# Attention heads of a two-layer diffusion block: projection blocks one step later, maxima first, other banks, early output projection

## The chip, the cores and the metric

One Trainium2 chip, one core of it. The metric is the time of one execution on the device in microseconds (us), median of several runs. All arithmetic is float32; a product of weights is made from three passes (see below). Engines: PE multiplies matrices (a weight load, PEld, goes with each product), DVE and ACT work on vectors, POOL is a third vector engine, SP only issues the transfers of weights (DMAs). Each has its own queue and runs it in order; they wait for each other by semaphores. Products land in eight banks (bank 0 to 7) of 128 x 512 numbers.

## The reference

Two layers over 256 context and 256 latent tokens of width 1024. Layer 0 is attention with compressed queries and keys/values, layer 1 a chunked state-space scan; a gated FFN follows each. The change lies in layer 0's attention alone:

```
proj = h @ w_in;  cq, ckv, kr = split(proj, [512, 768])
q  = rms_norm(cq)  @ w_uq      # 16 heads x (64 plain + 32 rotary)
kv = rms_norm(ckv) @ w_ukv     # 16 heads x (64 keys + 64 values)
q_rope, kr: rotated by position, latent tokens only
per head: s = (q k^T) / sqrt(96);  p = softmax(s);  o = p @ v
   latent queries see all 512 tokens, context queries the 256 of the context
out = concat(o) @ w_o          # 1024 x 1024
x = x + gate * out             # then norm and FFN
```

## The kernel before

Activations lie transposed (channels on partitions, tokens along the row). A weight block of 128 x 1024 (or 512) numbers comes by DMA into one of four `raw` buffers; ACT copies its high part into `w_hi` (`hi`, L574), DVE subtracts for `w_lo` (`lo`, L993), and PE makes three products for each of them (`three`, L1551 to L1553: low x high, high x high, high x low). The ring has four slots: a block's `hi` waits until the block four before is used (`w_used`), SP's load until its `w_lo` is written. Results of each sub-layer are split into high and low in the same way.

Layer 0's attention runs head by head. The queries and keys of four heads come from four projection blocks: K (keys of four heads, two halves of six products), C (rotary part of four queries, 12 products), A and B (plain part of two heads each, 12 products). `HEAD_BLOCKS` gives their order, K C A B for heads 0 to 3 and then A B C K for each group. Blocks 0 to 4 are done ahead of the loop, block i+5 in step i.

Step i of the loop (`head(i)`, written out for each engine in its own function) holds:

- PE: scores of head i+1 in three products (`scores`, L1737 and L1741; banks 0, 1, 4), transposes of head i's probabilities in three parts (`transpose_probs`, L1752 and L1756; banks 5, 6, 2), the swap of rotary halves in steps 2, 6, 10 (`swap`, L1723; bank 7), a projection block (bank 7; a K block in banks 5 and 6, whose halves first wait for the copies of the transposes there, `pt_out`), and the values of head i (`values`, L1768 and L1771; bank 3, after `pt_out` of the third part and after the low halves of head i-1, `o_lo`).
- ACT: exponentials of head i+1 (`exps`, L782 and L787) and copies of the transposed probabilities (`pt_split`, L799) by turns, copies of the projection block out of its bank (`project_out`: keys L751, rotary L756 and L761, plain L768), the next `hi`, the high halves of head i's output (L814).
- DVE: maxima of head i+1 (`maxes`, L1164 to L1170), inverses of the sums (`inverse`, L1178), the rotation in steps 2, 6, 10 (`rotate`, L1149 to L1157, reads bank 7), else a pair of matrix-vector operations for the modulation (`matvec`, L1070), the low halves of head i's output (L1195, reads bank 3), the next `lo`.
- POOL: three multiplies of the probabilities by the inverses (`scale_probs`, L460 to L464).
- SP: the load of the next head block or of an output projection block, and one vector-weight load.

After step 15 PE waits for the last low halves and makes the output projection: eight tiles of 128 channels, 24 products each; five over all tokens (banks 0 and 1 by turns), three in two halves. DVE adds each to the residual (L1222).

```
def head(i):                          # PE, before
    scores(i + 1, 0..2)
    transpose_probs(i, 0..2)          # for p < 2 of the step after a K block: wait k_out
    if i in ROPE_STEPS: swap(i + 4, bank[7])
    K: wait pt_out 3i+1; k_tile(b, 0, bank[5]); wait pt_out 3i+2; k_tile(b, 1, bank[6])
    else: q_tile(b, bank[7])          # b = i + 5
    values(i)
```

Of the kernel before, what the change touches and what calls it, by code (L numbers as in the profile page):

```python
# [27 lines left out]
CTX = 256  # L28
LAT = 256
# [73 lines left out]
HEAD_BLOCKS = [("K", 0), ("C", 0), ("A", 0), ("B", 0)] + [(kind, g) for g in range(1, 4) for kind in "ABCK"]  # L103
ROPE_STEPS = [b - 4 for b, (kind, g) in enumerate(HEAD_BLOCKS) if kind == "C" and g]
# [40 lines left out]
def program(nc, a, out):  # L145
# [9 lines left out]
    with ExitStack() as fixed:  # L155
# [407 lines left out]
        def _(act):  # L563
# [173 lines left out]

            def project_out(b, banks):
# [3 lines left out]
                if kind == "K":  # L742
                    for half in range(2):
                        if half:
                            act.wait_ge(w_used, HP + b + 1)
                        else:
                            act.wait_ge(k_mm, g + 1)
                        if g:
                            act.wait_ge(s_mm, 3 * h)
                        for u in range(2):  # L750
                            A(kf[0:64, 2 * half + u, :], banks[half][64 * u:64 * u + 64, :], ACT.Copy).then_inc(k_out, 1)  # L751
# [49 lines left out]
            def head(i):  # L801

                for p in (0, 1):
                    if i < 15:
                        exps(i + 1, p)
                    pt_split(i, p)
                pt_split(i, 2)
                if i < 15:
                    exps(i + 1, 2)
                if i + 5 < 16:  # L810
                    project_out(i + 5, (bank[5], bank[6]) if HEAD_BLOCKS[i + 5][0] == "K" else (bank[7],))
# [7 lines left out]
            project_out(3, (bank[2],))  # L819
            for p in range(3):  # L820
                exps(0, p)
            project_out(4, (bank[7],))
# [161 lines left out]
        def _(dve):  # L984
# [158 lines left out]
            def rotate(g, b):  # L1143
# [7 lines left out]
                V.tensor_tensor(rope_s[:, :], b[:, 0:LAT], tabv("sin", LAT), MUL).then_inc(rope_part, 1)  # L1151
# [27 lines left out]

            def head(i, v):  # L1180
                if i < 15:
                    maxes(i + 1, 0)
                    maxes(i + 1, 1)
                    inverse(i + 1, 0)
                    maxes(i + 1, 2)
                    inverse(i + 1, 1)
                if i in ROPE_STEPS:
                    rotate(HEAD_BLOCKS[i + 4][1], bank[7])
# [4 lines left out]
                for r in range(2):  # L1193
                    dve.wait_ge(o_hi, 2 * i + r + 1)
                    V.tensor_tensor(halves(Ol, i // 2, i % 2, r), bank[3][64 * r:64 * r + 64, 0:256].rearrange("p (s t) -> p s t", s=2),  # L1195
                                    halves(Oh, i // 2, i % 2, r).bitcast(f32), SUB).then_inc(o_lo, 1)
                if i + 5 < 16:
# [960 lines left out]
```

## Time and profile before

| | us |
|---|---|
| median of 3 runs | 1287.66 (1285.13 to 1290.57) |
| the profiled execution | 1290.45 |
| its span, first to last instruction | 1288.7 |
| busy PE / DVE / ACT / POOL | 1181.0 / 862.5 / 588.1 / 220.6 |
| mean granted TensorE clock | 0.963 |

The span is one profiled execution; sums made from its rows stand against 1290.45. Busy times say how full an engine is, not which wait decides; for that there is the chain of waits and, for one stretch, the timeline of each engine. A timeline row has the start, the duration, the engine and line, the operation and its shapes, how many were merged, and in brackets how long the engine was idle before it and who ended that. The granted clock is 1.00 at 2.4 GHz and 0.50 at 1.2 GHz.

### The profile page before, as it was taken

How to read it: one execution, taken by the hardware profiler on the slowest of the kernel's cores; microseconds unless marked ns; L12 is line 12 of the kernel's file. 1: busy time of each engine (PE TensorE's matmuls, PEld its weight loads, DVE VectorE, ACT ScalarE, POOL GpSimd, SP SyncE). 2: the span in 40 equal slices, each digit the busy share in tenths (PEclk: the TensorE clock that was granted, in tenths of full speed). 3: DMA queues.
4: the chain of work that ended last, by engine and by line, in shares of the span. 5: the costliest groups of instructions: out<-in, count | busy, mean ns of one | idle time of the engine just before them, and what ended most of it. 6: DMA issues, size and time to landing. Idle time of an engine off the chain costs nothing.

```text
span 1288.7 us, 19417 instructions
## 1 busy us (share of the span) xinstructions
PE 1181.0 (92%) x6954; PEld 984.0 (76%) x6954; DVE 862.5 (67%) x1311; ACT 588.1 (46%) x986; POOL 220.6 (17%) x174
## 2 busy tenths in 40 slices
PE   5799998788999999999998899999989798999997
PEld 3577666568988888878888778889544697999996
DVE  0886778766787777775664778784677655555454
ACT  3657777534432222222223565555533345655542
POOL 0102343422100000000112100010688421000011
PEclk9899999899999999999999999999989798999999
DMA  9532212131465555554542132226200043665562
GB/s 382 186 135 93 82 66 83 56 126 49 157 220 185 189 195 195 195 187 128 171 148 85 41 115 82 84 80 192 70 0 1 1 148 114 196 193 183 150 181 77
DMA packets 48173, 168.19 MB, mean 131 GB/s; under 512 B 5232, under 2 KB 6512, under 8 KB 47856
## 3 DMA queue, kind: packets, MB, share of 16 engines
q1 hardware_dynamic: 48112, 167.38, 39.0%
q8 instruction: 38, 0.62, 0.2%
q14 instruction: 23, 0.19, 0.0%
HBM read 166.31 MB, written 1.05 MB: 130 GB/s over the span
## 4 chain that ended last, share of the span: by engine, by line
PE 70%; DVE 14%; ACT 8%; issue 5%; DMA 1%; SPq 1%; POOL 1%; DVEq 0%; ACTq 0%; POOLq 0%
PE bank L1551 21%; PE bank L1553 20%; PE bank L1552 20%; DVE scratch L1355 5%; DVE w_lo L993 2%; DVE scratch L1470 1%; DMA raw<-in_w_in 1%; PE bank L1982 1%; PE bank L1970 1%; ACT scratch L869 1%; PE bank L1992 1%; ACT w_hi L574 1%; PE bank L1737 1%; ACT conv_in L866 1%; ACT probs_t L799 1%
## 5 line engine op out<-in xcount | busy, mean ns | idle before, releaser
L993 DVE TENSOR_TENSOR w_lo<-raw,w_hi 128x1024 fp32r<-128x1024 f32 (+1 forms) x226 | 269.1, 1193 | 169.8 <-ACT w_hi L574 169.6
L574 ACT ACTIVATE w_hi<-raw 128x1024 fp32r<-128x1024 f32 (+1 forms) x226 | 230.8, 1023 | 276.7 <-PE bank L1553 255.3
L1551 PE MATMUL bank<-ffn_h_lo,w_hi 128*128 128x256 f32 (+1 forms) x736 | 245.8, 334 | 8.2 <-DVE ffn_h_lo L1030 4.9
L1552 PE MATMUL bank<-ffn_h_hi,w_hi 128*128 128x256 f32 (+1 forms) x736 | 245.0, 333 | 0.0
L1553 PE MATMUL bank<-ffn_h_hi,w_lo 128*128 128x256 f32 (+1 forms) x736 | 245.0, 333 | 0.0
L1551 PEld LDWEIGHTS bank<-ffn_h_lo,w_hi 128*128 128x128 f32 x736 | 140.3, 191 | 23.4 <-issue 5.2
L1552 PEld LDWEIGHTS bank<-ffn_h_hi,w_hi 128*128 128x128 f32 x736 | 140.2, 191 | 14.6
L1553 PEld LDWEIGHTS bank<-ffn_h_hi,w_lo 128*128 128x128 f32 x736 | 140.2, 190 | 14.6
L433 POOL TENSOR_TENSOR scratch<-scratch 128x512 f32<-128x512 f32 (+1 forms) x24 | 37.4, 1559 | 606.8 <-ACT scratch L583 606.8
L1551 PE MATMUL bank<-ffn_hidden_lo,w_hi 128*128 128x256 f32 (+1 forms) x374 | 123.8, 331 | 5.7 <-DVE ffn_hidden_lo L1315 5.7
L1551 PE MATMUL bank<-ssd_h_lo,w_hi 128*128 128x256 f32 (+2 forms) x360 | 121.1, 336 | 7.6 <-DVE w_lo L993 4.6
L1552 PE MATMUL bank<-ffn_hidden_hi,w_hi 128*128 128x256 f32 (+1 forms) x374 | 123.5, 330 | 0.0
L1553 PE MATMUL bank<-ffn_hidden_hi,w_lo 128*128 128x256 f32 (+1 forms) x374 | 123.4, 330 | 0.0
L1552 PE MATMUL bank<-ssd_h_hi,w_hi 128*128 128x256 f32 (+2 forms) x360 | 118.5, 329 | 0.0
L1553 PE MATMUL bank<-ssd_h_hi,w_lo 128*128 128x256 f32 (+2 forms) x360 | 118.4, 329 | 0.0
L1355 DVE SCALAR_TENSOR_TENSOR scratch<-conv_in,par,scratch 128x512 f32<-128x512 f32 (+1 forms) x96 | 67.9, 707 | 28.6 <-ACT scratch L869 21.9
L1551 PEld LDWEIGHTS bank<-ffn_hidden_lo,w_hi 128*128 128x128 f32 x374 | 71.1, 190 | 13.5 <-DVE ffn_hidden_lo L1315 6.4
L1551 PEld LDWEIGHTS bank<-ssd_h_lo,w_hi 128*128 128x128 f32 (+1 forms) x360 | 69.4, 193 | 15.2 <-DVE w_lo L993 5.0
L1552 PEld LDWEIGHTS bank<-ffn_hidden_hi,w_hi 128*128 128x128 f32 x374 | 71.1, 190 | 7.0
L1553 PEld LDWEIGHTS bank<-ffn_hidden_hi,w_lo 128*128 128x128 f32 x374 | 71.2, 190 | 7.0
L1553 PEld LDWEIGHTS bank<-ssd_h_hi,w_lo 128*128 128x128 f32 (+1 forms) x360 | 69.2, 192 | 6.6
L1552 PEld LDWEIGHTS bank<-ssd_h_hi,w_hi 128*128 128x128 f32 (+1 forms) x360 | 69.4, 193 | 5.9
(266 smaller groups left out, 2172.3 us busy)
## 6 DMA issues: line engine op xcount, KB each, us to landing
raw<-in_w SPq DMA_DIRECT2D x120, 512.0 KB, 4.3
scratch<-in_vec_w SPq DMA_DIRECT2D x56, 512.0 KB, 3.5
vec_weights<-in_vec_w SPq DMA_DIRECT2D x24, 512.0 KB, 3.5
raw<-in_w_xbc SPq DMA_DIRECT2D x24, 512.0 KB, 3.5
ada_start<-in_ada_w SPq DMA_DIRECT2D x8, 1024.0 KB, 17.3
raw<-in_w_z SPq DMA_DIRECT2D x16, 512.0 KB, 3.6
raw<-in_w_so SPq DMA_DIRECT2D x16, 512.0 KB, 3.8
raw<-in_w SPq DMA_DIRECT2D x16, 384.0 KB, 3.8
```

What stands on the lines that cost most here:

```text
L433: nc.gpsimd.tensor_tensor(T[:, ACC[w], 0:n], before, T[:, (b + k) % 2, 0:n], ADD).then_inc(sq_used, 2 if k == 1 else 1)
L574: A(wh[s % RING][:, 0:c], raw[s % RING][:, 0:c], ACT.Copy).then_inc(w_hi, 1)
L799: A(dst, src, ACT.Copy).then_inc(pt_out, 1)
L866: A(up[:, u, :, 2:258], o[:, :].rearrange("p (s t) -> p s t", s=2), ACT.Copy).then_inc(conv_up, 1)
L869: A(acc, up[:, u, seg, 0:256], ACT.Identity, bias=par[:, ds(PAR["conv_b"] + t, 1)], scale=par[:, ds(PAR["conv_w"] + 5 * t, 1)]).then_inc(c ...
L993: V.tensor_tensor(wl[s % RING][:, 0:c], raw[s % RING][:, 0:c], wh[s % RING][:, 0:c].bitcast(f32), SUB).then_inc(w_lo, 1)
L1355: V.scalar_tensor_tensor(acc, up[:, u, seg, r:r + 256], par[:, ds(PAR["conv_w"] + 5 * t + r, 1)], acc, MUL, ADD).then_inc(conv_tap, 1)
L1470: last = V.scalar_tensor_tensor(T[:, 2 + h // 4, q], cbf[:, 4 * c + g, :], dt[:, 2 + c, GH * g + h:GH * g + h + 1], T[:, 4 + h // 4, q], M ...
L1551: mm(o, lh, rl, start=first, stop=False)
L1552: mm(o, lh, rh, start=False, stop=False)
L1553: return mm(o, ll, rh, start=False, stop=final)
L1737: last = mm(bank[p][:, :], qf[0:QKD, q, qs], kf[0:QKD, i % 4, :], start=True, stop=True)
```

## The change

The projection blocks move one step later: block i+4 in step i, in the order A C K B for each group; B of the last group falls into step 11. Ahead of the loop only four blocks are left, and the fourth, B of heads 2 and 3, stands behind head 0's scores and, on ACT, behind its exponentials. On DVE the two first maxima of head i+1 stand ahead of the low halves of head i-1's output (a new function `out_low`), which before stood at the end of step i-1. The swap writes the second half of bank 3, and PE waits for `o_lo` of the head before it and, before the values, for DVE's reading of it (`rope_part`). Both halves of a K block go to bank 7, the first ahead of the values, the second behind them, each copied by ACT from there (`k_half_out`); its weights' `hi` stays behind the second copy. The first output projection tile goes to bank 7 in three pieces within steps 12, 13 and 15 (`wo_part`: channels of heads 0 to 7, 8 to 11, 12 and 13), its rest after the loop.

```diff
@@ -100,8 +100,9 @@
-HEAD_BLOCKS = [("K", 0), ("C", 0), ("A", 0), ("B", 0)] + [(kind, g) for g in range(1, 4) for kind in "ABCK"]
-ROPE_STEPS = [b - 4 for b, (kind, g) in enumerate(HEAD_BLOCKS) if kind == "C" and g]
+HEAD_BLOCKS = [("K", 0), ("C", 0), ("A", 0), ("B", 0)] + [(kind, g) for g in range(1, 4) for kind in "ACKB"]
+ROPE_STEPS = [b - 3 for b, (kind, g) in enumerate(HEAD_BLOCKS) if kind == "C" and g]
+WO_PART = {12: (0, 4), 13: (4, 6), 15: (6, 7)}
 VEC_STEPS = [i for i in range(15) if i not in ROPE_STEPS]
@@ -735,20 +736,25 @@
+            def k_half_out(b, half, o):
+                g = HEAD_BLOCKS[b][1]
+                if half:
+                    act.wait_ge(w_used, HP + b + 1)
+                else:
+                    act.wait_ge(k_mm, g + 1)
+                if g:
+                    act.wait_ge(s_mm, 12 * g - 6 + 6 * half)
+                for u in range(2):
+                    A(kf[0:64, 2 * half + u, :], o[64 * u:64 * u + 64, :], ACT.Copy).then_inc(k_out, 1)
...
                     for half in range(2):
-                        if half:
-                            act.wait_ge(w_used, HP + b + 1)
-                        else:
-                            act.wait_ge(k_mm, g + 1)
-                        if g:
-                            act.wait_ge(s_mm, 3 * h)
-                        for u in range(2):
-                            A(kf[0:64, 2 * half + u, :], banks[half][64 * u:64 * u + 64, :], ACT.Copy).then_inc(k_out, 1)
+                        k_half_out(b, half, banks[half])
                 elif kind == "C":
@@ -800,15 +806,21 @@
+                kind = HEAD_BLOCKS[i + 4][0] if i + 4 < 16 else None
                 for p in (0, 1):
...
                 pt_split(i, 2)
+                if kind == "K":
+                    k_half_out(i + 4, 0, bank[7])
                 if i < 15:
                     exps(i + 1, 2)
-                if i + 5 < 16:
-                    project_out(i + 5, (bank[5], bank[6]) if HEAD_BLOCKS[i + 5][0] == "K" else (bank[7],))
+                if kind == "K":
+                    k_half_out(i + 4, 1, bank[7])
+                    hi(HP + i + 8, HP + i + 8)
+                elif kind:
+                    project_out(i + 4, (bank[7],))
                 act.wait_ge(o_mm, i + 1)
@@ -816,10 +828,9 @@
             project_out(2, (bank[5],))
-            project_out(3, (bank[2],))
             for p in range(3):
                 exps(0, p)
-            project_out(4, (bank[7],))
+            project_out(3, (bank[7],))
             for i in range(HEADS):
@@ -1148,7 +1159,7 @@
                 dve.wait_ge(q_perm, g + 1)
-                V.tensor_tensor(rope_s[:, :], b[:, 0:LAT], tabv("sin", LAT), MUL).then_inc(rope_part, 1)
+                V.tensor_tensor(rope_s[:, :], b[:, LAT:2 * LAT], tabv("sin", LAT), MUL).then_inc(rope_part, 1)
                 dve.wait_ge(rope_part, 2 * g + 2)
@@ -1177,29 +1188,35 @@
+            def out_low(i):
+                for r in range(2):
+                    dve.wait_ge(o_hi, 2 * i + r + 1)
+                    V.tensor_tensor(halves(Ol, i // 2, i % 2, r), bank[3][64 * r:64 * r + 64, 0:256].rearrange("p (s t) -> p s t", s=2),
+                                    halves(Oh, i // 2, i % 2, r).bitcast(f32), SUB).then_inc(o_lo, 1)
...
                     maxes(i + 1, 1)
+                if i:
+                    out_low(i - 1)
+                if i < 15:
                     inverse(i + 1, 0)
...
                 if i in ROPE_STEPS:
-                    rotate(HEAD_BLOCKS[i + 4][1], bank[7])
+                    rotate(HEAD_BLOCKS[i + 3][1], bank[3])
                 if v is not None:
...
                     inverse(i + 1, 2)
-                for r in range(2):
-                    dve.wait_ge(o_hi, 2 * i + r + 1)
-                    V.tensor_tensor(halves(Ol, i // 2, i % 2, r), bank[3][64 * r:64 * r + 64, 0:256].rearrange("p (s t) -> p s t", s=2),
-                                    halves(Oh, i // 2, i % 2, r).bitcast(f32), SUB).then_inc(o_lo, 1)
-                if i + 5 < 16:
-                    lo(HP + i + 9, HP + i + 9)
+                if i + 4 < 16:
+                    lo(HP + i + 8, HP + i + 8)
             lo(HP + 4, HP + 4)
-            rotate(0, bank[7])
-            for b in range(5, 8):
+            rotate(0, bank[3])
+            for b in range(5, 7):
                 lo(HP + b, HP + b)
@@ -1208,9 +1225,10 @@
             inverse(0, 2)
-            lo(HP + 8, HP + 8)
+            lo(HP + 7, HP + 7)
             for i in range(HEADS):
                 head(i, VEC_HEADS + VEC_STEPS.index(i) if i in VEC_STEPS else None)
+            out_low(15)
             dve.wait_ge(vec_bias, 1)
@@ -1291,7 +1309,7 @@
             for m in range(5):
-                add(WO + m + 1, m, m % 2, 0, 2, both)
+                add(WO + m + 1, m, m % 2 if m else 7, 0, 2, both)
                 lo(WO + m + RING, WO + m + RING)
@@ -1720,7 +1738,9 @@
                 pe.wait_ge(q_raw, g + 1)
-                mm(o[:, 0:LAT], tabv("swap"), qr[:, CTX:TOK], start=True, stop=True).then_inc(q_perm, 1)
+                if g:
+                    pe.wait_ge(rope_part, 2 * g)
+                mm(o[:, LAT:2 * LAT], tabv("swap"), qr[:, CTX:TOK], start=True, stop=True).then_inc(q_perm, 1)
@@ -1772,32 +1792,46 @@
             def head(i):
-                b = i + 5
+                b = i + 4
                 kind, g = HEAD_BLOCKS[b] if b < 16 else (None, None)
...
                 for p in range(3):
-                    if p < 2 and HEAD_BLOCKS[(b - 1) % 16][0] == "K" and b <= 16:
-                        pe.wait_ge(k_out, 4 * HEAD_BLOCKS[b - 1][1] + 2 * p + 2)
                     transpose_probs(i, p)
                 if i in ROPE_STEPS:
-                    swap(i + 4, bank[7])
+                    pe.wait_ge(o_lo, 2 * i)
+                    swap(i + 3, bank[3])
                 if kind == "A":
-                    pe.wait_ge(rope_part, 2 * g)
+                    pe.wait_ge(q_nope, 4 * g)
                     q_tile(b, bank[7])
-                elif kind == "B":
+                elif kind == "C":
                     pe.wait_ge(q_nope, 4 * g + 2)
                     q_tile(b, bank[7])
-                elif kind == "C":
-                    pe.wait_ge(q_nope, 4 * g + 4)
+                elif kind == "K":
+                    pe.wait_ge(q_raw, g + 1)
+                    k_tile(b, 0, bank[7])
+                elif kind == "B":
+                    pe.wait_ge(k_out, 4 * g + 4)
                     q_tile(b, bank[7])
-                elif kind == "K":
-                    pe.wait_ge(pt_out, 3 * i + 1)
-                    k_tile(b, 0, bank[5])
-                    pe.wait_ge(pt_out, 3 * i + 2)
-                    k_tile(b, 1, bank[6])
+                elif i in WO_PART:
+                    wo_part(*WO_PART[i])
+                if i in ROPE_STEPS:
+                    pe.wait_ge(rope_part, 2 * HEAD_BLOCKS[i + 3][1] + 2)
                 values(i)
+                if kind == "K":
+                    pe.wait_ge(k_out, 4 * g + 2)
+                    k_tile(b, 1, bank[7])
+            def wo_part(k0, k1):
+                pe.wait_ge(q_nope, HEADS)
+                pe.wait_ge(w_lo, WO + 1)
+                pe.wait_ge(o_lo, 4 * k1)
+                for k in range(k0, k1):
+                    w = slice(128 * k, 128 * k + 128)
+                    last = three(bank[7][:, :], wh[WO % RING][:, w], wl[WO % RING][:, w], Oh[:, k, :], Ol[:, k, :], k == 0, k == KD - 1)
+                return last
@@ -1806,21 +1840,19 @@
             q_tile(2, bank[5])
-            swap(1, bank[7])
-            q_tile(3, bank[2])
+            swap(1, bank[3])
             pe.wait_ge(kr_cp, 3)
...
                 scores(0, p)
-            pe.wait_ge(rope_part, 2)
-            q_tile(4, bank[7])
-            pe.wait_ge(q_nope, 4)
+            q_tile(3, bank[7])
+            pe.wait_ge(q_nope, 2)
             for i in range(HEADS):
...
-            pe.wait_ge(o_lo, 2 * HEADS)
-            for m in range(5):
-                if m >= 2:
+            wo_part(7, KD).then_inc(w_used, 1)
+            for m in range(1, 5):
+                if m >= 3:
                     pe.wait_ge(added, m - 1)
...
```

## Rows read from the trace of the kernel before

**Rows 1.** The page's section 4: the chain that ended last, by engine.
```profile
PE 70%; DVE 14%; ACT 8%; issue 5%; DMA 1%; SPq 1%; POOL 1%; DVEq 0%; ACTq 0%; POOLq 0%
```

**Rows 2.** Timeline of PE: start, duration, line, operation, operands, idle before; value products, output projection.
```profile
124.96 0.66 PE L1768 MATMUL bank<-probs_t,v 128*64 128x128 f32 x8 [1.02 <-ACT probs_t L799]
...
133.60 0.66 PE L1768 MATMUL bank<-probs_t,v 128*64 128x128 f32 x8 [0.23 <-ACT probs_t L799]
...
154.78 0.66 PE L1768 MATMUL bank<-probs_t,v 128*64 128x128 f32 x8
...
192.81 0.66 PE L1768 MATMUL bank<-probs_t,v 128*64 128x128 f32 x8
...
234.27 0.66 PE L1768 MATMUL bank<-probs_t,v 128*64 128x128 f32 x8 [3.18 <-ACT probs_t L799]
...
267.22 0.50 PE L1551 MATMUL bank<-mla_h_lo,w_hi 128*128 128x512 f32 x1 [1.39 <-DVE mla_h_lo L1195]
```

**Rows 3.** Timeline of PE: first scores in the loop's prologue, and one step.
```profile
111.72 1.88 PE L1737 MATMUL bank<-k_heads,q_heads 96*128 96x512 f32 x4
...
160.16 0.47 PE L1551 MATMUL bank<-c_normed_lo,w_hi 128*128 128x512 f32 x1
...
163.13 0.66 PE L1768 MATMUL bank<-probs_t,v 128*64 128x128 f32 x8
...
164.59 1.98 PE L1737 MATMUL bank<-k_heads,q_heads 96*128 96x512 f32 x4
```

**Rows 4.** Timeline of PE: waits for copied probabilities, in heads 2, 10 and 14.
```profile
141.93 0.50 PE L1551 MATMUL bank<-c_normed_lo,w_hi 128*128 128x512 f32 x1 [2.28 <-ACT probs_t L799]
...
220.93 0.50 PE L1551 MATMUL bank<-c_normed_lo,w_hi 128*128 128x512 f32 x1 [3.24 <-ACT probs_t L799]
...
259.40 0.66 PE L1768 MATMUL bank<-probs_t,v 128*64 128x128 f32 x8 [1.78 <-ACT probs_t L799]
```

**Rows 5.** Windows, PE: stretch, length, busy (count), granted clock, DMA share, GB/s.
```profile
143.00:146.00 3.00, 3.00 (x9) 0.52 0.03 8
...
236.00:241.00 5.00, 5.00 (x10) 0.50 0.31 105
```

**Rows 6.** Timeline of DVE: prologue, one step, last inverse.
```profile
113.67 0.69 DVE L993 TENSOR_TENSOR w_lo<-raw,w_hi 128x512 fp32r<-128x512 f32 x1 [1.00 <-ACT w_hi L574]
...
150.13 0.69 DVE L1164 TENSOR_REDUCE softmax_max<-bank 128x1 f32<-128x512 f32 x1
...
153.31 1.20 DVE L1070 SCALAR_TENSOR_TENSOR vec_products<-vec_weights,silu_c_rows 128x1024 f32<-128x1024 f32 x1
...
154.44 2.05 DVE L1070 SCALAR_TENSOR_TENSOR vec_weights<-vec_weights,silu_c_rows 128x1024 f32<-128x1024 f32 x1
...
156.43 0.15 DVE L1178 RECIPROCAL softmax_inv<-softmax_sum 128x2 f32<-128x2 f32 x1
...
157.26 0.88 DVE L1195 TENSOR_TENSOR mla_h_lo<-bank,mla_h_hi 64x256 fp32r<-64x256 f32 x2 [0.68 <-ACT mla_h_hi L814]
...
158.17 0.69 DVE L993 TENSOR_TENSOR w_lo<-raw,w_hi 128x512 fp32r<-128x512 f32 x1
...
261.63 0.15 DVE L1178 RECIPROCAL softmax_inv<-softmax_sum 128x2 f32<-128x2 f32 x1
```

**Rows 7.** Timeline of ACT: step of block C (head 1), and keys' copies in head 6.
```profile
130.45 0.78 ACT L782 ACTIVATE scratch<-bank,softmax_negmax,q_scale 128x512 f32<-128x512 f32 x1 [2.05 <-DVE softmax_negmax L1170]
...
134.49 0.63 ACT L756 ACTIVATE q_rope<-bank 128x512 f32<-128x512 f32 x1
...
136.90 0.63 ACT L574 ACTIVATE w_hi<-raw 128x512 fp32r<-128x512 f32 x1
...
184.57 1.21 ACT L751 ACTIVATE k_heads<-bank 64x512 f32<-64x512 f32 x2 [0.79 <-PE bank L1553]
```

**Rows 8.** Timeline of POOL: second and third multiply of one head.
```profile
153.47 1.95 POOL L462 TENSOR_TENSOR scratch<-scratch,softmax_inv 128x512 f32<-128x512 f32 x1 [0.23 <-DVE softmax_inv L1178]
...
156.66 1.04 POOL L464 TENSOR_TENSOR scratch<-scratch,softmax_inv 128x512 f32<-128x512 f32 x1 [1.25 <-DVE softmax_inv L1178]
```

## The prediction

> **What bounds the kernel now.** The chain of waits gives 70% of the span to PE [rows 1], so time is won only where PE waits, runs at the lower clock, or does work that another place could hide. I read the timeline of PE through the attention heads. The start of each head's value product marks a step: head 0's is at 124.96, head 1's at 133.60, and the output projection begins at 267.22 [rows 2]. A step whose PE queue is full runs from head 3's values at 154.78 to head 4's at 163.13, 8.35 us: values 1.46, then scores and transposes 3.92, and one projection block 2.97 [rows 2, 3]. Yet head 1 to 3 take 21.18 us, 3 to 7 38.03 and 7 to 11 41.46 [rows 2], where four full steps are 33.4. The excess stands in the key steps: there PE waits 2.28 and 3.24 us for the copy of transposed probabilities that frees banks 5 and 6 [rows 4], and after such a wait its granted clock is 0.52 for some 3 us (1.2 instead of 2.4 GHz), at worst 0.50 for 5 us in head 12's step, which follows a wait of 3.18 [rows 2, 5]. Waits of 1.78 us [rows 4] have no such stretch behind them.
>
> **Why PE waits there.** DVE, in one step (m is the start of the first maximum): m = 150.13, matrix-vector pair at m+3.2, last inverse at m+6.3, then it waits for ACT before the outputs' low halves at 157.26, and the weights' low half at 158.17 (0.69) [rows 6]. Exponentials start 0.92 after m (reduction 0.69, product 0.16, hand-overs); in the step of block C ACT begins them at 130.45, has them and the three copies done at 134.49, and its rotary copies and weight copy last to 137.53, m+8.0 [rows 7]. Only then come the outputs' high halves, behind them DVE's low halves and weights, and only then the next maxima. Values cannot begin before about m+4.07, since three copies must end.
>
> **The change, part by part.** Let t be the end of a value product. The next full PE step ends 8.35 later; the next m is the later of DVE free and t+0.97 (first score product).
>
> *Prologue.* Block A1 (12 products, 2.97 us) leaves the prologue for head 0's step, B0 goes behind head 0's scores. These start at 111.72 now [rows 3] and can start up to 2.97 earlier; by how much hardly matters, since DVE sets the next point. Its third low half at 113.67, which it waited 1.00 for and which takes it 0.6 to the next start, falls away [rows 6]: m of head 0 comes 1.6 earlier, and the same 1.6 to 1.7 passes to head 1's m and to values 0, 123.3 (124.96 now). Values 1 are then bound by PE: 1.46 + 3.92 + 2.97 later, 131.6, 1.9 before 133.60. B0, behind the scores, costs PE its 2.97 before head 1's scores, which wait for head 0's exponentials there anyway.
>
> *Maxima first.* The two maxima no longer stand behind the outputs' low halves; those (0.91 with the step) move between second maximum and first inverse, so the later inverses and the matrix-vector pair slip by 0.91. DVE's loop is 6.38 + 0.91 + 0.72 = 8.0, below PE's 8.35; with a weight block of 1024 columns some 8.6, above it (steps 8, 9 and 11).
>
> *One cost that is easy to miss.* The last inverse releases POOL's third multiply (1.04 alone, 1.95 for the second one beside the matrix-vector pair, whose second half takes 2.05 against 1.20) [rows 6, 8]. So a DVE operation with two operands in SBUF waits for a running POOL multiply. Before, the outputs' low halves covered that multiply; now the weights' low half follows the inverse. Where its ACT partner is done it wins; where it must wait for ACT (step 0 and the C steps) it meets POOL until m+8.5. Bounds 0 and 1.04 each; I take 0.5 in a C step and 0.9 in step 0. The C step is then 8.5 + 0.7 = 9.2 (9.8 with 1024 columns, where ACT itself ends at 8.45).
> The Trainium skill, page "SBUF — State Buffer", section "SBUF: two separate sides", says that the shared pair is an exclusive lock for a whole instruction, taken by GpSimd or by a VectorE instruction with two SBUF inputs. The trace agrees (1.95 against 1.04). Without the rule the sum would be some 2 us better.
>
> *Key steps.* The first half now goes to bank 7 right after the swap, without the copies' wait; the second after the values, when ACT has emptied bank 7. New waits: the swap into bank 3 waits for the low halves of the head before, m+2.6; the values wait until DVE's rotation has read it, m+4.85 (4.1, then two products of 0.4); all of PE's step is queued behind either. Step 2: t = 133.1, m = 136.8 (step 0's m of 119.2, then 8.4 with its collision, then 9.2), transposes end 137.0, swap at 139.4, first half (6 products, 1.5) to 141.35, rotation read 141.7, values to 143.2, second half 144.7. So 11.6 us from t to t, where PE alone would need 9.3. ACT's two copies (1.2 [rows 7]) and weights' high half (0.6), then DVE's low half (0.7) put m 2.6 after t, still inside PE's 6.88. Head 3: 151.6 (now 154.78). Steps 3 to 5: m falls back to 2.0 after t, the C step makes it 2.9, the swap waits 1.6, step 6 lasts 10.8. Head 7: 187.35 (now 192.81), 5.5 gained. Steps 8, 9 with 1024 columns bring m to 4.0 after t, so the swap of step 10 waits 2.65, step 10 lasts 11.9; m is then 3.5 after t, and values 11 wait for it: 224.9 (now 234.27), 9.4 gained.
>
> *Clock.* Two new waits, 2.4 in step 2 and 2.65 in step 10, are as long as those with a fall behind them [rows 4, 5]. A fall costs about 1.4 to 1.6 (3.2 us of PE work at half speed). Bounds: none, and both (and a third in step 6). I take one, since the longer of the two stands between the rows of 2.28 and 3.24, both with a fall, and the shorter comes with more work close around it.
>
> *Last heads.* Step 11 gets B3, step 12 half of output tile 0 (12 products, 2.97), step 13 six, step 15 three. Step 11 to 12 is 8.6 (DVE), then 7.33, 7.33 (DVE without a weight block), the last inverse to the output projection 5.6 as now (261.63 to 267.22 [rows 2, 6]). In 12 the clock stretch of 0.50 should go, as PE has only 0.3 us to wait before; the six and three products lie in waits that PE has anyway. The projection's remainder starts 32.0 after values 11, now 32.95: 10.3 gained without a fall, 8.9 with one.
>
> *Output tile 0.* 21 of 24 products leave the path: 12 take 2.97 with their start [rows 3], so about 0.23 each, 4.9 us. Everything behind shifts whole: tiles 1 to 7 are a full PE queue as before, and SP issues the same loads in the same order, each released by the low half of the block four before it; a block's low half is now written one step later but also used one step later for A, B and C alike, so no load comes closer to its use. POOL's queue is not touched.
>
> **Sum.** 8.9 + 4.9 = 13.8 us. The profiled execution took 1290.45 us (span 1288.7), so 1276.6; it lies 2.8 above the median of 1287.66, so against that 1273.9. No fall: 1272.5; two: 1275.3.
>
> **Rivals.**
> (a) *The waits close up better*: no fall and no POOL collision. For: 1.78 us did no harm; the lock's 0.5 is an estimate. Against: 2.28 did. 15.2 + 2 = 17.2, 1270.5. Chance 0.12.
> (b) *DVE becomes the bound*: the 0.91 moved ahead of the inverses, plus collisions, make every full step 8.75 instead of 8.35 and no key step falls below 12. For: DVE's loop has only 0.35 to spare. Against: the old loop included 0.7 to 2.7 of waiting for ACT. Ten steps by 0.4 lost of the forecast, 9.8 gained: 1278. Chance 0.13.
> (c) *It does only half of what it says*: ACT's order (high halves behind rotary copies) still sets the loop, and the key steps stay at 12.8; only moved PE work counts, 1.9 + 4.9 = 6.8: 1280.9. Against: the exponentials waited 2.05 for DVE [rows 7], so ACT was not last. Chance 0.08.
> (d) *Slower: TensorE's clock stays at 1.2 GHz.* Each step now has a wait, mostly at the swap or the values. For: falls exist. One full step at half clock costs some 6 us more (block, values and the scores' part of the 3.92 double). The gain of 13.8 is used up from the third whole step on; four (24 us) give 1298. Against: the longest low stretch now is about 6 us, after 3.18 of waiting, and it ended under plain work. Chance 0.04.
> The forecast keeps 0.63.
>
> **Numbers.** Least difference that a measurement of this kernel tells from none: 0.5%, 6.4 us. Faster by more: forecast, (a), (b) and half of (c), 0.91; within: the rest of (c) and a part of (d), 0.06; slower 0.03. Range 1265 to 1281: below, (a) with the spread of the runs (2.5); above, (b) and (c).
>
> **What would show it.** Right: no wait for banks 5 and 6 in steps 2, 6, 10; value products 3, 7, 11 near 151.6, 187.4, 225 to 226; output tile 0 done near 259; a short wait at the swap, longest in step 10; DVE's next maximum before the outputs' low half; no stretch of 0.50 in step 12. Wrong: PE waiting elsewhere over 1 us in the plain steps, low clock over whole steps, or the tiles after output tile 0 starting to wait for weights.

## The result

| | median, us | four runs | ratio to before (95% interval) |
|---|---|---|---|
| before | 1286.74 | 1285.13 to 1290.57 | |
| changed | 1272.38 | 1271.95 to 1273.40 | 0.9885 (0.9861 to 0.9909) |

The change gains 14.4 us; 13.8 were forecast. Each trace is one execution. That of the changed kernel took 1271.95 us, that of the kernel before 1290.45, which is 3.7 above its median, so the two traces are 18.5 apart: 16.6 up to the end of output tile 0, the other 1.9 in stages that the change does not touch. From the output projection to the end (with its first 21 products taken off where they stand there) the traces of this case need 1014 to 1018 us, so differences of 2 us there are the spread of single executions.

PE's timeline of the changed kernel, with the rows that answer to [rows 2 to 4]: value products L1788, swap L1743, first scores L1757, first products of blocks L1569.

```profile
110.91 1.96 PE L1757 MATMUL bank<-k_heads,q_heads 96*128 96x512 f32 x4 [1.17 <-ACT q_heads L774]
...
123.92 0.66 PE L1788 MATMUL bank<-probs_t,v 128*64 128x128 f32 x8 [0.70 <-ACT probs_t L805]
...
132.26 0.66 PE L1788 MATMUL bank<-probs_t,v 128*64 128x128 f32 x8
...
139.16 0.70 PE L1743 MATMUL bank<-q_rope,tab 128*128 128x256 f32 x2 [1.28 <-DVE mla_h_lo L1195]
...
141.29 0.66 PE L1788 MATMUL bank<-probs_t,v 128*64 128x128 f32 x8
...
142.75 0.50 PE L1569 MATMUL bank<-c_normed_lo,w_hi 128*128 128x512 f32 x1
...
144.25 1.88 PE L1757 MATMUL bank<-k_heads,q_heads 96*128 96x512 f32 x4
...
151.04 0.66 PE L1788 MATMUL bank<-probs_t,v 128*64 128x128 f32 x8
...
186.02 0.66 PE L1788 MATMUL bank<-probs_t,v 128*64 128x128 f32 x8
...
210.24 0.70 PE L1743 MATMUL bank<-q_rope,tab 128*128 128x256 f32 x2 [1.90 <-DVE mla_h_lo L1195]
...
222.92 0.66 PE L1788 MATMUL bank<-probs_t,v 128*64 128x128 f32 x8 [0.73 <-ACT probs_t L805]
...
252.48 0.66 PE L1788 MATMUL bank<-probs_t,v 128*64 128x128 f32 x8
...
255.49 0.47 PE L1569 MATMUL bank<-mla_h_lo,w_hi 128*128 128x512 f32 x1 [1.48 <-DVE mla_h_lo L1195]
```

The values of heads 3, 7 and 11 stand at 151.04, 186.02 and 222.92 instead of 154.78, 192.81 and 234.27 [rows 2]; PE waits in the key steps for the swap (1.28 and 1.90 here, 0.78 in step 6), not for banks 5 and 6, and its granted clock is 1.00 from head 0's values to the output projection. Windows of PE (stretch, length, busy, granted clock, DMA share, GB/s) behind the longest of these waits:

```profile
210.00:211.00 1.00, 0.76 (x3) 1.00 0.00 0
211.00:213.00 2.00, 1.96 (x18) 1.00 0.00 0
213.00:216.00 3.00, 3.00 (x26) 1.00 0.02 5
```

DVE in steps 0 to 2, 7 and 11 of the changed kernel, answering to [rows 6] (weights' low half L1004, first maximum L1175, last inverse L1189, outputs' low halves L1195):

```profile
126.59 1.38 DVE L1004 TENSOR_TENSOR w_lo<-raw,w_hi 128x512 fp32r<-128x512 f32 x1 [0.28 <-ACT w_hi L575]
127.89 0.68 DVE L1175 TENSOR_REDUCE softmax_max<-bank 128x1 f32<-128x512 f32 x1
...
134.73 0.15 DVE L1189 RECIPROCAL softmax_inv<-softmax_sum 128x2 f32<-128x2 f32 x1
135.92 0.69 DVE L1004 TENSOR_TENSOR w_lo<-raw,w_hi 128x512 fp32r<-128x512 f32 x1 [1.03 <-ACT w_hi L575]
136.53 0.68 DVE L1175 TENSOR_REDUCE softmax_max<-bank 128x1 f32<-128x512 f32 x1
...
138.23 0.88 DVE L1195 TENSOR_TENSOR mla_h_lo<-bank,mla_h_hi 64x256 fp32r<-64x256 f32 x2
...
188.73 0.67 DVE L1004 TENSOR_TENSOR w_lo<-raw,w_hi 128x512 fp32r<-128x512 f32 x1
...
226.02 2.04 DVE L1004 TENSOR_TENSOR w_lo<-raw,w_hi 128x1024 fp32r<-128x1024 f32 x1 [0.16 <-ACT w_hi L575]
```

POOL's third multiplies beside them:

```profile
126.38 1.04 POOL L465 TENSOR_TENSOR probs<-probs,softmax_inv 128x512 f32<-128x512 f32 x1 [1.24 <-DVE softmax_inv L1189]
...
134.96 1.04 POOL L465 TENSOR_TENSOR scratch<-scratch,softmax_inv 128x512 f32<-128x512 f32 x1 [1.25 <-DVE softmax_inv L1189]
...
188.88 1.41 POOL L465 TENSOR_TENSOR scratch<-scratch,softmax_inv 128x512 f32<-128x512 f32 x1 [1.25 <-DVE softmax_inv L1189]
...
225.94 1.04 POOL L465 TENSOR_TENSOR scratch<-scratch,softmax_inv 128x512 f32<-128x512 f32 x1 [1.24 <-DVE softmax_inv L1189]
```

POOL's times are rougher than the others. In step 0 the low half began 0.21 after POOL's multiply and took 1.38 instead of 0.69; in step 1 it came when POOL was just done, and took 0.69. In step 7, at 188.73, the low half began first and took 0.67, and POOL's multiply took 1.41 instead of 1.04. In step 11 the low half of 1024 columns began 0.08 after POOL's multiply and took 2.04, where the others of its size took 1.23.

### The profile page after: what moved, and what is told of

Same layout as the page of the kernel before. It is cut to its first block, busy times and chain, and to the rows that moved or that the text cites. A ratio compares the mean times of both kernels' runs of the same rounds, so it can differ in the third digit from the quotient of the medians.

```text
span 1270.2 us, 19422 instructions
## 1 busy us (share of the span) xinstructions
PE 1172.1 (92%) x6954; PEld 977.9 (77%) x6954; DVE 863.5 (68%) x1311; ACT 589.7 (46%) x986; POOL 223.7 (18%) x174
## 4 chain that ended last, share of the span: by engine, by line
PE 77%; DVE 12%; ACT 4%; issue 3%; DMA 1%; POOL 1%; SPq 1%; DVEq 0%; ACTq 0%; POOLq 0%
PE bank L1569 23%; PE bank L1570 23%; PE bank L1571 23%; DVE w_lo L1004 2%; DVE scratch L1488 1%; DMA raw<-in_w_in 1%; PE bank L2002 1%; PE bank L2014 1%; DVE softmax_max L1175 1%; ACT w_hi L575 1%; PE bank L2024 1%; DVE scratch L1373 1%; DVE mla_h_lo L1195 1%; PE bank L2033 1%; DVE vec_weights L1081 1%
## 5 line engine op out<-in xcount | busy, mean ns | idle before, releaser
L1004 DVE TENSOR_TENSOR w_lo<-raw,w_hi 128x1024 fp32r<-128x1024 f32 (+1 forms) x226 | 270.6, 1200 | 179.8 <-ACT w_hi L575 179.6
L1569 PE MATMUL bank<-ffn_h_lo,w_hi 128*128 128x256 f32 (+1 forms) x736 | 246.2, 335 | 8.2 <-DVE ffn_h_lo L1041 4.9
L1569 PEld LDWEIGHTS bank<-ffn_h_lo,w_hi 128*128 128x128 f32 x736 | 140.5, 191 | 23.8 <-issue 5.2
L1571 PEld LDWEIGHTS bank<-ffn_h_hi,w_lo 128*128 128x128 f32 x736 | 140.5, 191 | 14.4
L1569 PE MATMUL bank<-ffn_hidden_lo,w_hi 128*128 128x256 f32 (+1 forms) x374 | 124.3, 332 | 5.7 <-DVE ffn_hidden_lo L1333 5.7
L1569 PE MATMUL bank<-ssd_h_lo,w_hi 128*128 128x256 f32 (+2 forms) x360 | 120.7, 335 | 8.0 <-DVE w_lo L1004 4.8
L1569 PEld LDWEIGHTS bank<-ffn_hidden_lo,w_hi 128*128 128x128 f32 x374 | 71.0, 190 | 13.7 <-DVE ffn_hidden_lo L1333 6.4
L1569 PEld LDWEIGHTS bank<-ssd_h_lo,w_hi 128*128 128x128 f32 (+1 forms) x360 | 68.8, 191 | 16.2 <-DVE w_lo L1004 5.2
L1081 DVE SCALAR_TENSOR_TENSOR matvec_products<-scratch,silu_c_rows 128x1024 f32<-128x1024 f32 x56 | 73.7, 1316 | 0.0
```

Of the source, the lines that this page charges most:

```text
L1004: V.tensor_tensor(wl[s % RING][:, 0:c], raw[s % RING][:, 0:c], wh[s % RING][:, 0:c].bitcast(f32), SUB).then_inc(w_lo, 1)
L1081: V.scalar_tensor_tensor(dst, buf, 1.0, crow[:, s, :], MUL, MUL, accum_out=m).then_inc(done, 1)
L1569: mm(o, lh, rl, start=first, stop=False)
L1571: return mm(o, ll, rh, start=False, stop=final)
```

## The experiments

Steps between value products, from the traces, in us (head 1 to 2 is key step 2, and so on; the total is the median):

| kernel | 1-2 | 2-3 | 5-6 | 6-7 | 9-10 | 10-11 | 11-12 | 12-13 | total |
|---|---|---|---|---|---|---|---|---|---|
| before | 12.75 | 8.43 | 12.87 | 8.34 | 13.84 | 8.80 | 10.49 | 7.24 | 1286.7 |
| changed | 9.03 | 9.75 | 8.53 | 9.75 | 9.65 | 10.55 | 9.12 | 7.50 | 1272.4 |
| e1, no early tile | 9.02 | 9.74 | 8.52 | 9.75 | 9.65 | 10.54 | 9.12 | 8.80 | 1278.7 |
| e2, lows behind | 10.12 | 10.90 | 10.12 | 12.46 | 11.09 | 13.35 | 9.98 | 7.17 | 1285.3 |
| e3, old banks | 10.33 | 8.34 | 9.82 | 8.34 | 12.80 | 8.34 | 8.35 | 7.41 | 1272.1 |
| e4, swap later | 11.44 | 10.19 | 11.21 | 9.90 | 12.64 | 11.55 | 9.11 | 7.50 | 1283.5 |
| e5, before + maxima first | 9.58 | 8.35 | 9.08 | 8.35 | 10.62 | 8.43 | 8.80 | 7.17 | 1275.9 |
| e6, before + early tile | 12.88 | 8.36 | 11.34 | 8.60 | 13.84 | 8.80 | 7.39 | 7.26 | 1278.7 |
| e7, blocks later only | 12.73 | 8.36 | 11.33 | 8.61 | 13.84 | 8.79 | 9.73 | 9.67 | 1288.7 |
| e8, half before swap | 8.35 | 9.75 | 7.97 | 9.74 | 8.95 | 10.54 | 9.11 | 7.50 | 1272.1 |
| e9, before + both | 9.58 | 8.35 | 9.08 | 8.35 | 10.62 | 8.41 | 7.48 | 7.27 | 1270.1 |
| e10, e8 + late halves | 8.35 | 9.74 | 7.97 | 9.75 | 8.95 | 9.75 | 8.35 | 7.17 | 1270.2 |
| e11, changed again | 9.02 | 9.75 | 8.52 | 9.74 | 9.62 | 10.53 | 9.12 | 7.49 | 1272.4 |
| e12, e9 + late halves | 9.56 | 8.34 | 9.08 | 8.34 | 8.78 | 8.34 | 7.17 | 7.17 | 1268.0 |

**e1: no early tile.**

```diff
-WO_PART = {12: (0, 4), 13: (4, 6), 15: (6, 7)}
+WO_PART = {}
-            wo_part(7, KD).then_inc(w_used, 1)
+            wo_part(0, KD).then_inc(w_used, 1)
```

> The changed kernel with output tile 0 made whole after the loop (still in bank 7), no pieces in steps 12, 13 and 15. Theory: 21 products of 0.233 us come back onto the path, +4.9 us, so about 1277; heads 12 to 15 keep their times within 0.5 us, since DVE sets them. Rival: the pieces had lengthened steps 12 to 15 by about what they save, then within 1 us of 1272.4.

Measured 1278.69 (1278.03 to 1280.07), ratio to before 0.9936 (0.9915 to 0.9958): 6.3 above the changed kernel. That is more than the 4.9, and heads 12 to 13 did not keep their time as expected (8.80 against 7.50). Without the pieces PE waits 3.49 us in step 12, and a stretch of lower clock follows; another stands in the last values (L1788 took 1.12 for eight products, 0.66 in the changed kernel). The last values, and a window behind the wait of step 12, in this kernel:

```profile
252.80 1.12 PE L1788 MATMUL bank<-probs_t,v 128*64 128x128 f32 x8 [0.69 <-ACT probs_t L805]
```

```profile
233.00:238.00 5.00, 5.00 (x25) 0.76 0.30 105
```

**e2: the outputs' low halves back behind their own step.**

```diff
-                if i:
-                    out_low(i - 1)
...
                     inverse(i + 1, 2)
+                out_low(i)
                 if i + 4 < 16:
                     lo(HP + i + 8, HP + i + 8)
```

> The changed kernel with the outputs' low halves back at the end of their own step, ahead of the weights' low half and of the next maxima. Theory: in a C step ACT ends the high halves 8.8 us after the first maximum, so the next maximum comes 10.7 after it instead of 8.7; in the key step PE waits some 2.6 us at the values (and falls to the lower clock), and after it again 1.3: about +4 us per key step, 1281 to 1285 in all, the swap without a wait. Rival: PE's full queue covers it, +2 us at most.

Measured 1285.34 (1284.38 to 1289.02), ratio 0.9993 (0.9977 to 1.001). With this one part taken back 13 of the 14.4 us are gone, though blocks, banks and early tile are all as changed. The first maximum of step 2 starts 6.0 after head 1's values (138.19 to 132.19) instead of 4.3. PE, then DVE, with head 2's output from 147.64 on, and ACT beside it:

```profile
142.31 0.66 PE L1786 MATMUL bank<-probs_t,v 128*64 128x128 f32 x8 [2.67 <-DVE rope_sin L1162]
...
153.21 0.66 PE L1786 MATMUL bank<-probs_t,v 128*64 128x128 f32 x8 [1.08 <-ACT probs_t L805]
...
180.74 0.66 PE L1786 MATMUL bank<-probs_t,v 128*64 128x128 f32 x8 [2.68 <-DVE rope_sin L1162]
```

```profile
138.19 0.69 DVE L1175 TENSOR_REDUCE softmax_max<-bank 128x1 f32<-128x512 f32 x1
...
147.64 0.87 DVE L1195 TENSOR_TENSOR mla_h_lo<-bank,mla_h_hi 64x256 fp32r<-64x256 f32 x2 [2.93 <-ACT mla_h_hi L826]
148.44 0.68 DVE L1004 TENSOR_TENSOR w_lo<-raw,w_hi 128x512 fp32r<-128x512 f32 x1
149.14 0.69 DVE L1175 TENSOR_REDUCE softmax_max<-bank 128x1 f32<-128x512 f32 x1
```

```profile
145.47 1.21 ACT L749 ACTIVATE k_heads<-bank 64x512 f32<-64x512 f32 x2 [0.96 <-PE bank L1569]
...
147.23 0.79 ACT L826 ACTIVATE mla_h_hi<-bank 64x256 fp32r<-64x256 f32 x2
```

DVE stands 2.93 us waiting for ACT's high halves while the next maxima could be taken (the scores begin at 145.28). The high halves come so late because ACT first waits for the second half of the K block, copies it and makes the weights' high half. Taking the order back costs 13.0 us here, and e5 below gains 11.3 by the same edit on the kernel before; the two intervals overlap, so that it costs more here is not shown. I expected a fall of the clock behind the wait of 2.67 in step 2; there is none (1.00 from 142 to 146), but there is one behind the 2.68 of step 6.

**e3: K blocks in banks 5 and 6 again.**

```diff
-                    k_tile(b, 0, bank[7])
+                    pe.wait_ge(pt_out, 3 * i + 1)
+                    k_tile(b, 0, bank[5])
+                    pe.wait_ge(pt_out, 3 * i + 2)
+                    k_tile(b, 1, bank[6])
...
-                if kind == "K":
-                    pe.wait_ge(k_out, 4 * g + 2)
-                    k_tile(b, 1, bank[7])
```

(ACT's two copies follow the third exponentials, and the transposes of the next step wait for them, as in the kernel before.)

> The changed kernel with the K blocks' halves back in banks 5 and 6, both ahead of the values, with the waits for the copied probabilities. Theory (maxima decide, not the banks): the copies end 2.3 and 3.4 us after the first maximum, before or with the swap's wait of 2.6, so the key steps last as long as now (10.0 to 11.5 us from scores to scores) and the time stays within 1.5 us of 1272.4. Rival (banks decide, the reading I gave the change in the prediction): waits of 2.3 us and a fall of the clock come back, +3 to 4 us per key step, 1282 to 1284.

Measured 1272.09 (1271.18 to 1272.81), ratio 0.9882 (0.9847 to 0.9917). The banks are worth nothing that can be measured: the time only moves from the key step to the one behind it (10.33 and 8.34 against 9.03 and 9.75). Step 10 alone is dearer, with a swap wait of 2.20 and a stretch of lower clock behind it:

```profile
209.14 0.70 PE L1742 MATMUL bank<-q_rope,tab 128*128 128x256 f32 x2 [2.20 <-DVE mla_h_lo L1194]
```

```profile
210.00:214.00 4.00, 4.00 (x12) 0.57 0.00 0
```

**e4: the swap waits longer.**

```diff
                     pe.wait_ge(o_lo, 2 * i)
+                    pe.wait_ge(nmax, 4 * i + 8)
                     swap(i + 3, bank[3])
```

> The changed kernel with the swap in steps 2, 6 and 10 held until the third maximum's products, 1.4 us later than now: PE's waits there become about 2.7, 2.2 and 3.3 us. Theory (a wait of this length brings the lower clock): a stretch of 0.5 follows in steps 2 and 10 at least, +1.2 per step for the wait and +1.4 per fall, 1278 to 1280. Rival (the falls of before had another cause): no stretch of 0.5, +3.6 us, 1276.

Measured 1283.48 (1274.17 to 1286.44, ten executions), ratio 0.9948 (0.9917 to 0.9979). In the trace the waits are 2.72, 2.22 and 3.33, and behind the first two and within the third the clock falls to 0.50. The key steps are 2.4, 2.7 and 3.0 longer, of which 1.4 is the added wait:

```profile
140.66 0.67 PE L1743 MATMUL bank<-q_rope,tab 128*128 128x256 f32 x2 [2.72 <-issue]
...
178.50 0.88 PE L1743 MATMUL bank<-q_rope,tab 128*128 128x256 f32 x2 [2.22 <-issue]
...
217.42 1.19 PE L1743 MATMUL bank<-q_rope,tab 128*128 128x256 f32 x2 [3.33 <-issue]
```

```profile
142.00:144.00 2.00, 2.00 (x7) 0.50 0.01 4
...
180.00:182.00 2.00, 2.00 (x7) 0.50 0.03 8
...
218.00:221.00 3.00, 3.00 (x8) 0.50 0.00 0
```

The median lies 3 us above what I expected, and its executions are spread over 12 us, where the other changed kernels here spread over 2 to 6 and the kernel before over almost 9. The executions form two groups, and the mean granted clock on record for each execution tells them apart: 0.962 to 0.965 in the six that took 1281.97 to 1286.44 us, the traced one among them, and 0.971 or 0.972 in the four that took 1274.17 to 1276.36. So the same program, with the same added waits, had falls in some executions and few or none in others. Without them it lies 2 to 4 us above the changed kernel, which is what the rival expected (1276). In which steps the untraced executions differ is not known.

**e5: the kernel before, with the maxima first and nothing else.** Its edit is the hunk at line 1177 of the change (`out_low` behind the second maximum).

> The kernel before with one edit: the two maxima of head i+1 ahead of the low halves of head i-1's output. Theory (this order is most of the gain): the maxima come some 2 us earlier in the steps behind a C block, the waits for banks 5 and 6 shrink from 2.3 to 3.2 us to under 1, their clock stretches go: 3 to 4 us per key step, 1275 to 1278. Rival (the blocks' place and the banks are needed for it): 3 us gained at most, 1284.

Measured 1275.87 (1272.86 to 1278.74), ratio 0.9904 (0.9873 to 0.9934): 11.3 us from this one edit. In key step 2 PE's wait for bank 5 is 0.54 instead of 2.28 [rows 4]; in step 10 it is 1.57 instead of 3.24, where I expected under 1. Step 11, which has no block, still waits 2.81 with a stretch of 0.57 behind.

```profile
140.44 0.50 PE L1558 MATMUL bank<-c_normed_lo,w_hi 128*128 128x512 f32 x1 [0.54 <-ACT probs_t L799]
```

```profile
222.00:226.00 4.00, 4.00 (x26) 0.57 0.04 10
...
255.00:260.00 5.00, 4.83 (x11) 0.50 0.01 3
```

This trace is the slowest of the four executions (1278.74, granted clock 0.965; the fastest took 1272.86 at 0.972). It holds one more low stretch, from about 250 to 261, across the last values and into the output projection, though PE waited no longer than 1.63 us at a time from step 12 on.

**e6: the kernel before, with the early tile and nothing else** (`WO_PART = {11: (0, 4), 12: (4, 6), 15: (6, 7)}`, bank 7).

> The kernel before with output tile 0 begun in steps 11 (12 products), 12 (6) and 15 (3). Theory: 4.9 us off the path, and as step 11 has work in its wait of 3.18 us, the stretch of 0.50 in step 12 goes too, another 2 to 3 us: 1279 to 1280. Rival: only the 4.9, the stretch stays: 1282.

Measured 1278.70 (1275.79 to 1280.15), ratio 0.9926 (0.9903 to 0.9949), 8.5 us. Head 11 to 12 falls from 10.49 to 7.39: the filled wait takes the clock stretch with it. Those 3.1 and the 4.9 are 8.0 of the 8.5. Head 5 to 6 is 1.5 shorter too (11.34 against 12.87), but that is no work of the edit: PE's wait there is 2.28, as in the trace before (2.27), and this time the clock did not fall behind it.

**e7: blocks one step later, and nothing else** (e1, e2 and e3 together).

> The changed kernel with three of its parts taken back: no early tile, low halves of the outputs at the old place, K blocks in banks 5 and 6. What is left is the order A C K B one step later, the shorter prologue and the swap in bank 3. Theory: 2 us from the prologue, 2 to 3 from B3 filling step 11 (no stretch of 0.50 in step 12), the key steps as before: 1282 to 1283. Rival: the shift alone gains nothing, 1286 to 1287.

Measured 1288.67 (1286.55 to 1291.84), ratio 1.0015 (1.0002 to 1.0029). The prologue's gain is in the trace (values 0 at 123.37 against 124.96), but the lower clock comes back elsewhere: step 12 has no block now, and PE waits 4.10 for its values and runs at 0.50 behind. My expectation of 4 us was wrong: B3 filled step 11, and step 12 became the empty one.

**e8: the first half of the K block ahead of the swap, the rotary products ahead of the third maximum.**

```diff
-                if i in ROPE_STEPS:
-                    pe.wait_ge(o_lo, 2 * i)
-                    swap(i + 3, bank[3])
...
                     k_tile(b, 0, bank[7])
+                    pe.wait_ge(o_lo, 2 * i)
+                    swap(i + 3, bank[3])
```

> The changed kernel with the K block's first half ahead of the swap (its 1.5 us fill the swap's wait), and DVE's two rotary products ahead of the third maximum, so that they free bank 3 earlier. Theory: the values of heads 2, 6 and 10 are then bound by the copied probabilities, 0.7 us earlier each, 2 us in all: 1270.5. Rival: the later third maximum delays the third exponentials and the gain is given back, 1272.5.

Measured 1272.06 (1271.08 to 1273.15), ratio 0.9882 (0.9855 to 0.9909). In the heads the expected gain is there (9.03, 8.53, 9.65 became 8.35, 7.97, 8.95, 2.0 us in all); in the total it is not (1270.5 was expected). In the two traces the stages behind the heads took 1016.2 against 1014.7, and 2 us are within what they vary; whether the gain is real in the total stays open.

**e9: the kernel before with both edits** (e5 and e6 together), **e10: e8 with late halves, e12: e9 with late halves, e11: the changed kernel again**, all on one chip. "Late halves" means that the high and low halves of output projection blocks 2 and 3 are made behind the loop. The edit, in e12:

```diff
-                if b + 4 < 16 + 4:
+                if b + 4 < 16 + 2:
                     hi(HP + b + 4, HP + b + 4)
...
             sqrt_table(1)
+            hi(WO + 2, WO + 2)
+            hi(WO + 3, WO + 3)
...
-                if i + 5 < 16:
+                if i < 9:
                     lo(HP + i + 9, HP + i + 9)
...
             out_low(15)
+            lo(WO + 2, WO + 2)
+            lo(WO + 3, WO + 3)
```

> The kernel before with two edits only: the two maxima ahead of the low halves of the outputs, and output tile 0 begun in steps 11, 12 and 15. Theory (these two carry the whole gain; later blocks, shorter prologue and other banks add nothing): 11.3 + 4.9, and the stretch at half clock behind step 11's wait of 2.81 goes too, so 1270 to 1272, the same as the changed kernel. Rival: the block shift is worth its 2 us of prologue and the filled step 11, so this one ends 2 to 4 us behind the changed kernel.

> The kernel with the half block ahead of the swap and the early rotary products, and besides the high and low halves of output projection blocks 2 and 3 made after the loop instead of in steps 10 and 11. Theory: the wait of 0.7 us ahead of head 11's values goes (10.54 to 9.75) and head 11 to 12 falls from 9.1 to 8.4, so 1.5 us in the heads; with the 1.9 of the half block 3 us in all against the changed kernel, 1269 to 1270. Rival: the two halves after the loop hold up output tile 2 or the loads behind them, and nothing is left.

> The kernel before with the two edits and the halves of output projection blocks 2 and 3 made after the loop. Theory: DVE's steps 10 to 12 shorten by 0.5 each, 1 to 1.5 us against the version with the two edits alone, 1269 to 1271. Rival: no change against it, since PE's queue is full there.

> The changed kernel as it is, beside the three others on one chip, to compare them with it: 1272.4 within 1 us.

| | median | executions | ratio to before |
|---|---|---|---|
| e9 | 1270.08 | 1268.96 to 1270.79 | 0.9869 (0.9847 to 0.9890) |
| e10 | 1270.19 | 1268.76 to 1270.70 | 0.9872 (0.9851 to 0.9893) |
| e12 | 1268.00 | 1265.67 to 1268.43 | 0.9850 (0.9828 to 0.9872) |
| e11 | 1272.44 | 1269.50 to 1273.87 | 0.9883 (0.9863 to 0.9904) |

Two edits on the kernel before reach at least what the whole change reaches; the remaining parts bring nothing on top. The trace of e9 has a low stretch in its last heads that the changed kernel has not, again behind waits of 1.64, 1.62 and 1.63; e12, with 1.55, 1.54 and 1.63 in the same places, has none:

```profile
248.00:251.00 3.00, 3.00 (x21) 0.50 0.80 322
```

The late halves give e10 its expected 1.6 in the heads against e8 (10.54 and 9.11 became 9.75 and 8.35). The late halves take the steps 9 to 12 of e9 from 10.62, 8.41, 7.48 to 8.78, 8.34, 7.17, and e12 beats both kernels: 18.3 us (1.4% of the median) under the kernel before and 4.4 under the changed kernel on the same chip, with no execution of the one inside the range of the other. Against e9 it gains 2.1, more than the 1 to 1.5 expected. Its output projection starts at 249.19:

```profile
249.19 0.47 PE L1563 MATMUL bank<-mla_h_lo,w_hi 128*128 128x512 f32 x1 [1.48 <-DVE mla_h_lo L1187]
```

## Why the prediction was right, and where not

- **Prologue**, 1.9 forecast: right. Values 0 and 1 at 123.3 and 131.6 were forecast; they are at 123.92 and 132.26, in a trace whose first K block starts 0.66 later (100.75 against 100.09).
- **Maxima first**: the timing was right. The maximum of step 2 was put 2.6 before the swap; it stands at 136.53, the swap at 139.16. What I credited it with was too little: I described it as an edit that lets the next point be set earlier, and named the other banks as what takes away the waits for copied probabilities. e3 and e5 say that this order does both, since banks 5 and 6 came free late only because the exponentials began late. The sum did not suffer, as it ran through all edits at once.
- **The cost that is easy to miss**, 0.9 in step 0 and 0.5 in each C step: half right. Step 0 paid 0.69. The C steps paid nothing: the last inverse came at m+6.84, not at the m+7.2 that the forecast's own numbers give (6.3 and 0.91), so POOL was done when the weights' high half came. The rows show why. Of the 0.91 only 0.56 reached the first inverse (it stands 2.38 after m, before 1.82), since the low halves take 0.79 there and fill a short wait that DVE had before that inverse. The two products behind the third maximum still run into POOL's first multiply, but less: 0.45 for the two, against 0.58 in the trace of before. Step 1 of the changed kernel, and below it the kernel before:

```profile
131.17 0.45 DVE L1181 TENSOR_TENSOR softmax_negmax<-softmax_max,q_neg 128x1 f32<-128x1 f32 x2
```

```profile
132.14 0.58 DVE L1170 TENSOR_TENSOR softmax_negmax<-softmax_max,q_neg 128x1 f32<-128x1 f32 x2
```

That step 0 paid less and the C steps nothing is most of the 0.7 to 1.1 by which each key step was forecast too long (scores to scores 11.6, 10.8 and 11.9; measured 10.53, 10.04 and 11.16). But step 11 paid, where the forecast had nothing: the low half took 2.04 instead of 1.23, and head 11 to 12 lasted 9.12 instead of the 8.6 forecast. The late halves of e10 take this away (8.35).
- **Clock**, one fall forecast in step 10: wrong, none. The swap waits were 1.28, 0.78 and 1.90 instead of 2.4, 1.6 and 2.65, for the reason just given. With waits of 2.72, 2.22 and 3.33 in the trace of e4, 0.3 to 0.7 longer than mine, there are three falls, but four of its ten executions went almost without. So shorter waits made the falls rarer; a wait of a given length does not decide it, and one fall as a fixed term of 1.4 us was more exact than the kernel is.
- **Output tile 0**, 4.9: right for the products. e1 shows 6.3 and e6 8.5, because the pieces also keep the clock up in the step that has no block.
- **The sum**: 13.8 against 14.4 by the medians, but 16.6 by the traces up to tile 0. The heads' part was 2.8 too small in the traces (11.7 from [rows 2] to 255.49, against 8.9): the key steps 2.6 and the fall 1.4, less 0.7 for the later first block and 0.6 for the last heads (32.6 from values 11 to the projection's remainder, forecast 32.0). That the medians agree within 0.6 is therefore partly luck: the sum was made from a trace of the kernel before that lies 3.7 above its median and held more low clock than most of its executions (granted clock 0.963, in most of the others 0.967 or 0.968), and the forecast took the whole gain from it over to the median. By its mechanism the course was rival (a)'s, no fall and almost no collision, though its 17.2 is above the medians' 14.4; (b) and (c) are excluded by key steps under 10 us from values to values (10.0 to 11.2 from scores to scores), (d) by the granted clock of 0.971 over the span (0.963 before).

Two small slips in the forecast's last lines change nothing: its chances for "faster" add up to 0.92, not 0.91, and rival (a) less 2.5 gives 1268, not 1265, for the lower end of the range.

The parts do not add up: maxima first 11.3, early tile 8.5, blocks later -1.5 and banks about 0 make 18.3, the whole 14.4. The two edits alone (e9) make 16.2 of their 19.8. Half of the missing 3.6 is seen in the traces: head 11 to 12 gains 1.7 in e5 and 3.1 in e6, but 3.0 in e9, since both edits take away the clock stretch of step 12 or part of it. The rest is within the intervals.

## What to carry to other kernels

When an engine's queue holds a wait for a slow partner ahead of work that others are waiting for, put the work first, where nothing that the wait holds up is needed soon. Here that one exchange of two maxima with the outputs' low halves was worth 11.3 us alone (e5), and 13.0 of the 14.4 were lost without it (e2); the later blocks, the shorter prologue and the other banks added nothing (e3, e7, e9). In the last steps of a loop, where blocks run out, give TensorE any later work that is ready: here it saved its own 4.9 us and the low clock behind that step's wait (e1, e6). Halves of weights that are needed only after the loop belong after it, if the engine that sets the loop's pace makes them (e12 against e9: 2.1 us). And look at the granted clock of every execution before a difference of a few us is explained from one trace.

## What the runs showed of the hardware

- The lower clock does not follow from a wait's length alone. Waits of 2.20 (e3) and 2.22 (e4) had it behind them, one of 2.67 in e2's step 2 had not (clock 1.00 from 142 to 146), the next of 2.68 in the same trace had. In e6 a wait of 2.28 had it in step 2 and another of 2.28 had not in step 6. In e5 and e9 it came in the last heads behind waits of 1.55 to 1.64, and in the changed kernel and e12 waits of 1.54 to 1.63 in the same places passed without it.
- The same program can run with or without such falls: e4 took 1274.2 to 1276.4 us at a mean granted clock of 0.971 to 0.972, and 1282.0 to 1286.4 at 0.962 to 0.965.
- A DVE subtraction with both operands in SBUF took 1.38 instead of 0.69 when it began 0.21 after a POOL multiply of 1.04, and ended 0.55 after POOL did; one of 1024 columns took 2.04 instead of 1.23 in the same position. When the subtraction began 0.15 before the multiply, it took 0.67 and the multiply 1.41. This agrees with the Trainium skill, page "SBUF — State Buffer", section "SBUF: two separate sides", which says that of the two the one that starts first holds the shared port pair for its whole instruction.
